# Squares of two norms added up by SBUF-to-SBUF transfers instead of by POOL

## The reference

```python
x = x + 0.5 * swiglu(rms_norm(x, ffn1_norm), ffn1_w1, ffn1_w3, ffn1_w2)
h = rms_norm(x, mix_norm)                 # the mixer's norm
proj = h @ w_in                           # then two kinds of attention, gates
...
x = x + (g_mla * y_mla + g_swa * y_swa) @ w_out
x = x + 0.5 * swiglu(rms_norm(x, ffn2_norm), ffn2_w1, ffn2_w3, ffn2_w2)
return rms_norm(x, final_norm)

def rms_norm(x, g):
    return x * rsqrt(mean(x * x, axis=-1) + EPS) * g
```

## Time and profile before

| | |
|---|---|
| median of three runs | 1145.99 us |
| the profiled execution | 1146.43 us |
| its span | 1144.7 us |
| PE busy | 1124.9 us (98%) |
| DVE busy | 574.6 us (50%) |
| ACT busy | 398.0 us (35%) |
| POOL busy | 170.6 us (15%) |
| additions of squares by POOL (L395) | 29, 45.1 us in all |
| mean data rate of the DMA engines | 92 GB/s |

### The profile page before, as it was taken

The page is one execution under the profiler, slowest core; times in us unless marked ns, Lnnn a source line. Parts: engine busy times, 40 slices in busy tenths (PEclk is TensorE's granted clock), DMA queues, the critical chain, the costliest instruction groups (busy, mean ns, idle before and its releaser), DMA issues.

```text
span 1144.7 us, 14986 instructions
## 1 busy us (share of the span) xinstructions
PE 1124.9 (98%) x5256; PEld 920.4 (80%) x5256; DVE 574.6 (50%) x883; ACT 398.0 (35%) x694; POOL 170.6 (15%) x136
## 2 busy tenths in 40 slices
PE   7999999999999999999999999999999999999996
PEld 5888888888888888777777788888888888888896
DVE  6644344443446436886555554445453344434544
ACT  5322222222225224684344432342231223212342
POOL 4111001100113202330000002331110011101123
PEclk9999999999999999999999999999999999999998
DMA  6234422332324231212212222232232322332222
GB/s 219 92 94 109 119 92 97 103 94 92 100 79 119 90 109 59 71 38 74 74 57 73 73 93 92 95 108 82 102 92 92 103 99 92 92 105 97 78 70 74
DMA packets 33582, 105.70 MB, mean 92 GB/s; under 512 B 3888, under 2 KB 7376, under 8 KB 33536
## 3 DMA queue, kind: packets, MB, share of 16 engines
q1 hardware_dynamic: 33104, 104.29, 27.7%
q0 software_dynamic: 192, 0.78, 0.6%
q10 hardware_dynamic: 240, 0.05, 0.0%
HBM read 102.22 MB, written 2.88 MB: 92 GB/s over the span
## 4 chain that ended last, share of the span: by engine, by line
PE 95%; DVE 2%; ACT 1%; POOL 1%; issue 0%; DMA 0%; SPq 0%; DVEq 0%; POOLq 0%; ACTq 0%
PE bank L1206 29%; PE bank L1207 29%; PE bank L1208 29%; PE bank L1326 2%; PE bank L1358 1%; PE bank L1383 1%; PE bank L1510 1%; PE bank L1512 1%; PE bank L1511 1%; PE bank L1317 1%; PE bank L1368 1%; DVE x L1182 0%; DMA x<-in_x_t 0%; PE bank L1267 0%; DVE w_lo L804 0%
## 5 line engine op out<-in xcount | busy, mean ns | idle before, releaser
L1206 PE MATMUL bank<-xg_hi,w_hi 128*128 128x512 f32 x1024 | 407.5, 398 | 8.0 <-DVE xg_lo L811 7.2
L1208 PE MATMUL bank<-xg_hi,w_lo 128*128 128x512 f32 x1024 | 400.6, 391 | 0.0
L1207 PE MATMUL bank<-xg_lo,w_hi 128*128 128x512 f32 x1024 | 400.5, 391 | 0.0
L545 ACT ACTIVATE w_hi<-staged 128x1024 fp32r<-128x1024 f32 x184 | 195.1, 1060 | 560.8 <-PE bank L1208 560.8
L804 DVE TENSOR_TENSOR w_lo<-staged,w_hi 128x1024 fp32r<-128x1024 f32 x184 | 226.9, 1233 | 99.1 <-ACT w_hi L545 98.9
L1206 PEld LDWEIGHTS bank<-xg_hi,w_hi 128*128 128x128 f32 x1024 | 193.2, 189 | 55.2 <-issue 12.3
L1208 PEld LDWEIGHTS bank<-xg_hi,w_lo 128*128 128x128 f32 x1024 | 193.2, 189 | 41.2
L1207 PEld LDWEIGHTS bank<-xg_lo,w_hi 128*128 128x128 f32 x1024 | 193.5, 189 | 39.1 <-issue 0.7
L415 POOL TENSOR_TENSOR h_lo<-hid,h_hi 128x512 f32 x44 | 70.9, 1611 | 565.3 <-ACT h_hi L568 537.0
L1206 PE MATMUL bank<-h_hi,w_hi 128*128 128x512 f32 x304 | 118.4, 389 | 0.2 <-POOL h_lo L415 0.2
L1207 PE MATMUL bank<-h_lo,w_hi 128*128 128x512 f32 x304 | 118.3, 389 | 0.0
(11 more groups left out here) (151 smaller groups left out, 1040.2 us busy)
## 6 DMA issues: line engine op xcount, KB each, us to landing
staged<-in_ffn_w SPq DMA_DIRECT2D x119, 512.0 KB, 3.3
staged<-in_w_gate SPq DMA_DIRECT2D x16, 512.0 KB, 3.2
staged<-in_w_in SPq DMA_DIRECT2D x15, 512.0 KB, 3.3
staged<-in_ffn_w SPq DMA_DIRECT2D x16, 384.0 KB, 3.1
staged<-in_w_ob SPq DMA_DIRECT2D x8, 512.0 KB, 3.2
staged<-in_w_out SPq DMA_DIRECT2D x8, 512.0 KB, 3.2
x<-in_x_t SPq DMA_DIRECT2D x8, 256.0 KB, 5.9
staged<-in_w_oa SPq DMA_DIRECT2D x4, 512.0 KB, 3.2
```

The costliest lines, as they stand in the source:

```text
L545: nc.scalar.activation(w_hi[:, u % SPLIT, :], staged[:, u % STAGED, :], ACT.Copy).then_inc(hi_done, 1)
L1206: nc.tensor.matmul(o, wh, hi, start=start, stop=False)
L1207: nc.tensor.matmul(o, wh, lo, start=False, stop=False)
L1208: return nc.tensor.matmul(o, wl, hi, start=False, stop=stop)
```

## The change

For the mixer's norm and the second feed-forward's norm, POOL no longer adds `sq` to `acc`. It issues a transfer from `sq` to `acc` that adds at its goal, waits until the transfer has landed, and then raises `acc_done` itself. The other norms are left as they are.

```diff
         sq_done, acc_done, acc_clear, acc_landed = ...
+        X_SENT = (NORM_MIX, NORM_X2)
...
+            def send_square(n, t, i=0):
+
+                s = sq_base[n] + t
+                landed = X_SENT.index(n) * KD + t + 1
+                pool.wait_ge(acc_clear, n + 1)
+                pool.wait_ge(sq_done, s + 1 + 4 * i)
+                pool.dma_start(acc[:, n % 2, :], sq[:, s % 2, :], accum_op=ALU.add).then_inc(acc_landed, 16)
+                pool.wait_ge(acc_landed, 16 * landed + 64 * i)
+                pool.sem_inc(acc_done, 1)
...
                 if n is not None:
                     clear_acc(n)
-                    loop(pool, 2, lambda i: [add_square(n, t, i) for t in range(4)], first=1)
+                    loop(pool, 2, lambda i: [send_square(n, t, i) for t in range(4)], first=1)
...
             clear_acc(NORM_X2)
-            loop(pool, 2, lambda i: [add_square(NORM_X2, t, i) for t in range(4)], first=1)
+            loop(pool, 2, lambda i: [send_square(NORM_X2, t, i) for t in range(4)], first=1)
```

More of the change, by code:

```diff
@@ L217, in trunk_layer @@
         xg_hi_done, xg_ready = sem("xg_hi_done"), sem("xg_ready")
-        sq_done, acc_done, acc_clear = sem("sq_done"), sem("acc_done"), sem("acc_clear")
+        sq_done, acc_done, acc_clear, acc_landed = sem("sq_done"), sem("acc_done"), sem("acc_clear"), sem("acc_landed")
         ss_ready, var_step, var_ready, root_ready = (
```

## The result

| | before | changed |
|---|---|---|
| median | 1145.92 us (7 runs, 1144.72 to 1146.54) | 1148.47 us (7 runs, 1148.26 to 1149.71) |
| profiled execution: span | 1144.7 us | 1146.7 us |

The ratio of changed to before is 1.0027, with a 95% interval of 1.0017 to 1.0036. It compares the means of the runs (3.1 us apart); the medians differ by 2.5 us. The change costs that. The time lies inside the range given, but past the 0.2% that I called no change and past the 1148.3 us above which I had called myself wrong. So the likeliest case was missed by little, and rival 1 is what happened.

The account below looks back on a forecast made before the run. PE was taken as the bound, busy 1124.9 of 1144.7 us, hiding POOL's additions. Removed 0 and added 0 at L = 4.4 left the profiled execution at 1146.4 us, the median forecast at 1146.3; range 1144.3 to 1160.

Parts of the forecast that it names:

- the likeliest case: Whole kernel: L up to 4.90 and no visible change, 1144.5 to 1148.3 us; chance 0.53.
- rival 1: Mixer's norm: PE's sum waits for the eighth landing; 1148.6 to 1160 us, chance 0.24; beyond that 0.12.
- L: Time from one transfer to the next in the chain, from POOL's issue to its raising of the semaphore.
- (a): Mixer's norm, chain's end: PE needs it at 387.0; cover gone at L = 4.61 us.
- (b): Second feed-forward's norm, chain's end: squares come further apart; cover gone at L = 5.50 us.
- The threshold: Mixer's norm: L at which eight transfers use up the cover before PE's sum, 36.9 / 8 = 4.61 us.
- L = 4.4: Each transfer: 2.7 us plain, 0.8 POOL's way, 0.5 second read, about 0.4 weight loads.
- (c): Mixer's norm: ACT's eighth square waits for the sixth landing; L = 4.55 free, PE stalls only past 5.4 us.
- The price of 0.8 us for each 0.1 of L: Mixer's norm: once the cover is gone at L = 4.61 us, each 0.1 us of L costs 0.8 us.
- Rival 2: POOL's issues: DVE holds them up by 1.23 us each, L 5.6, about 1155 us; chance 0.07.
- The estimate by the page: Each transfer: about 2.0 us plus bytes at 436 GB/s, L 2.6 or 3.2 us; chain never falls behind.
- Rivals 3 and 4: DVE and POOL undisturbed, at most 0.6 us faster; weight loads late, cost 0. Chance: inside 0.53, the first mostly.

Follow-up runs that it names:

- the halves: The changed kernel with each transfer cut into two halves of 256 columns, one waiting for the other; 1197.41 us, 1.0449 against the kernel before.

## Why the prediction was off by this much

- **What would be seen.** The forecast was no visible change, with 0.53; rival 1 had 0.24 from 1148.6 us on, just above what was measured. The range held because it was wide enough for rival 1, not because L was right.
- **Nothing to gain, and the place of a loss: right.** Removing POOL's additions gained nothing (the second norm alone: 0.9996). The loss sits at the mixer's norm and none at the second, as (a) and (b) had it.
- **The threshold: right in kind, 0.6 us too high.** I gave the chain 36.9 us from the end of the first square. POOL issues the first transfer only 0.6 us after that end (349.86 to 350.45; its addition began after 0.14), and from the issue on there are 36.3 us, so L = 4.54 and not 4.61. It lasted 38.9 us in the changed kernel (sum 2.6 us later) and 38.7 with the mixer's alone (2.4, and 1.7 for the low clock in the traced run). With the bias loads early it was over after 34.0 us, ahead of PE, and nothing was lost.
- **L = 4.4: the step that failed**, in the term for traffic beside the transfer. The rest of the sum (2.7 + 0.8 + 0.5 = 4.0 us) was near: a quiet transfer takes 3.85. That is partly luck, since its parts were off in opposite directions: 2.90 for the copy where I had 3.5, and 0.96 for the addition where I had 0.5. For the traffic I took 0.4 us, the mean share of the engines (0.39) times 1 us. It measured 4.86 - 3.85 = 1.0 us as a mean: 0 to 1.3 in most steps, and 3.5 in the third, beside the bunch of weight loads. A mean share was the wrong measure, since the loads run in bursts (slices at nine tenths and more next to slices at nothing in the rows above), and a transfer meets a burst or misses it. The eight bias loads stood in the trace of before, and I had not asked what waits behind them on SP.
- **(c), ACT's wait: wrong.** I tested it at the eighth square only and with even steps. With the long third step ACT is held from the fifth square on. PE loses 0.8 us and more for `w_lo` before the sum. I had looked at `xg`, which is needed late, and not at the copy of weights behind it, which is needed in the next product. What (c) ended with held: such a stall is not added to the wait in (a), since the chain sets the end.
- **The price of 0.8 us for each 0.1 of L** is right up to the sum ((4.86 - 4.54) x 8 = 2.6 us, as measured; the table above has it up to 29.3 us). For large excesses the whole kernel loses more than that, since PE then also runs at the lower clock behind the sum (in the halves granted 0.78 in 400 to 430 us, with a wait of 7.0 us at the sum).
- **Rival 2, DVE holding up POOL's issue: out.** All 16 issues last 0.85 to 0.92 us, with DVE busy half the time. The block of which the Trainium skill's box tells (SBUF — State Buffer, the box on DVE blocking DMA) shows in no row here; whether other operations of DVE would cause it, no run tested.
- **The estimate by the page** of the Trainium skill (DMA: Bandwidth & Descriptors, Anatomy of one DMA) was 2.6 us, or 3.2 with both reads counted. From issue to landing the quickest plain copy took 2.3 us and the quickest adding transfer 3.2, so this case agrees with it roughly. From start to start it is 2.90 and 3.85, and the estimate has no term for the traffic that decided here.
- **Rivals 3 and 4** show nothing to be gained or lost, as forecast (the second norm alone: 0.9996). The loads came late for ACT only with the bias loads doubled (1.9 us).

No version found here is faster than the kernel before. Those with the loss removed are level with it.

## What to carry to other kernels

A chain of dependent transfers is as long as all its steps together, and the slow ones are found by asking which other transfers start from the same event or pile up behind a busy queue, not by the engines' mean share. When a POOL operation of 1.6 us becomes a transfer with a wait, it takes 3.9 us in quiet and 7.4 or more beside a bunch of loads. Set that against the distance between two links and against the whole cover, and follow each buffer's wait to everything behind it on the waiting engine. Before moving work off an engine, ask who waits for it; here nobody did.

## What the runs showed of the hardware that was not expected

- An adding transfer keeps POOL 0.86 us with its issue, a plain one 0.54 us, for the same 128 rows of 2 KB.
- From start to start, in quiet: 256 KB adding 3.85 us, 128 KB adding 2.9 us, 256 KB plain 2.90 us.
- An adding transfer in the same step as one load is as short as a quiet one (3.85 us) when their data pass at different times; beside 2.60 MB, five loads' bytes, it took 9.4 us.
- The same chain of eight squares in halves, with the same program, took 58.3 us in one trace and 63.2 in another.
- A wait of 1.57 us by TensorE was followed by about 3 us at the lower clock in one execution, a wait of 2.9 us in another kernel likewise; waits of 1.17 and 1.20 us were followed by none.
